# The sample group's cached keys are stored page by page, and the new keys get a buffer and a matmul of their own

## The reference, cut to what matters

```
# per sample: 512 cached keys (4 pages of 128, found by page_table) and 8 new keys
k_all = concatenate([past_k, k]); v_all = concatenate([past_v, v])
s = einsum(q, k_all) * DA_DK**-0.5 + bias        # 8 heads, 2 maps, 8 queries, 520 keys
p = softmax(where(dist >= 0, s, NEG_INF))
o = (p[:, 0] - lam * p[:, 1]) @ v_all            # then RMSNorm per head
```

## Time and profile before

| | us |
|---|---|
| median of 3 runs | 1562.69 |
| lowest and highest | 1562.01, 1567.64 |
| span of the profiled execution | 1563.0 |
| PE busy in it | 1482.6 (95%) |
| DVE, ACT, POOL busy | 615.1, 468.7, 72.6 |

### The profile page before, as it was taken

One profiled execution on the slowest core, in us unless ns is written; L12 is line 12 of the kernel. 1 busy time (PEld: TensorE's weight loads), 2 busy tenths in 40 slices (PEclk: granted clock), 3 DMA queues, 4 the chain that ended last, 5 costly groups with the idle time before them and its releaser, 6 DMA issues.

```text
span 1563.0 us, 26015 instructions
## 1 busy us (share of the span) xinstructions
PE 1482.6 (95%) x10030; PEld 1337.4 (86%) x10030; DVE 615.1 (39%) x940; ACT 468.7 (30%) x817; POOL 72.6 (5%) x133
## 2 busy tenths in 40 slices
PE   4999999988799999999999999999999999999996
PEld 3999965535599999999999336999999999999995
DVE  5212222257832234533334443335634444443223
ACT  4222210026743323333334115333332222222221
POOL 2000010021100001200010000000000000000000
PEclk9999999999999999999999999999999999999998
DMA  5436178720112433123256640222222222223232
GB/s 186 141 103 227 54 226 250 237 75 21 40 55 81 137 96 103 54 81 122 83 209 182 232 155 1 81 81 85 77 81 81 81 87 87 81 81 95 81 94 74
DMA packets 78422, 171.79 MB, mean 110 GB/s; under 512 B 5565, under 2 KB 39613, under 8 KB 77350
## 3 DMA queue, kind: packets, MB, share of 16 engines
q1 hardware_dynamic: 76614, 164.05, 33.0%
q0 software_dynamic: 1760, 7.08, 1.3%
HBM read 161.65 MB, written 11.82 MB: 111 GB/s over the span
## 4 chain that ended last, share of the span: by engine, by line
PE 61%; issue 28%; DVE 5%; DMA 3%; ACT 1%; SPq 1%; POOL 0%; DVEq 0%; POOLq 0%; ACTq 0%
PE acc L1579 43%; PE ps L1702 4%; PE acc L1675 3%; PE ps L1866 2%; PE acc L1885 2%; PE ps L1750 2%; DMA w_raw<-w_stream 1%; DMA k_pg<-cache_k 1%; DVE logit_p L1139 1%; PE acc L1936 1%; PE acc L1771 1%; ACT w_hi L613 1%; DVE a_p L1159 1%; DVE w_lo L960 1%; PE acc L1761 1%
## 5 line engine op out<-in xcount | busy, mean ns | idle before, releaser
L960 DVE TENSOR_TENSOR w_lo<-w_raw,w_hi 128x1024 fp32r<-128x1024 f32 x188 | 231.0, 1229 | 590.8 <-ACT w_hi L613 590.2
L1579 PE MATMUL acc<-h_hi,w_hi 128*128 128x288 f32 x1856 | 399.7, 296 | 7.6 <-DVE h_lo L995 4.5
L1579 PE MATMUL acc<-h_lo,w_hi 128*128 128x288 f32 x1856 | 396.5, 294 | 0.0
L1579 PE MATMUL acc<-h_hi,w_lo 128*128 128x288 f32 x1856 | 396.3, 294 | 0.0
L613 ACT ACTIVATE w_hi<-w_raw 128x1024 fp32r<-128x1024 f32 x188 | 198.5, 1056 | 360.5 <-PE acc L1579 355.6
L1579 PEld LDWEIGHTS acc<-h_hi,w_hi 128*128 128x128 f32 x1856 | 297.2, 188 | 10.1 <-issue 5.2
L1579 PEld LDWEIGHTS acc<-h_hi,w_lo 128*128 128x128 f32 x1856 | 297.9, 188 | 0.0
L1579 PEld LDWEIGHTS acc<-h_lo,w_hi 128*128 128x128 f32 x1856 | 297.8, 188 | 0.0
L1579 PE MATMUL acc<-o_hi,w_hi 128*128 128x288 f32 x384 | 82.2, 295 | 2.0 <-ACT zmT L882 1.2
L1579 PE MATMUL acc<-o_hi,w_lo 128*128 128x288 f32 x384 | 82.1, 294 | 0.0
L1579 PE MATMUL acc<-o_lo,w_hi 128*128 128x288 f32 x384 | 81.7, 294 | 0.0
(11 more groups left out here) (242 smaller groups left out, 1576.7 us busy)
## 6 DMA issues: line engine op xcount, KB each, us to landing
w_raw<-w_stream SPq DMA_DIRECT2D x188, 512.0 KB, 3.5
v_pg<-cache_v SPq DMA_DIRECT2D x28, 512.0 KB, 4.7
k_pg<-cache_k SPq DMA_DIRECT2D x16, 512.0 KB, 6.3
k_odd<-cache_k SPq DMA_DIRECT2D x16, 512.0 KB, 6.4
km_pg<-mem_k SPq DMA_DIRECT2D x8, 1024.0 KB, 5.1
vm_pg<-mem_v SPq DMA_DIRECT2D x8, 1024.0 KB, 5.0
x_sb<-xT SPq DMA_DIRECT2D x8, 576.0 KB, 4.7
kT_out<-kT POOLq DMA_DIRECT2D x1, 2304.0 KB, 10.6
```

Source lines behind the costliest of these rows:

```text
L960: nc.vector.tensor_tensor(w_lo[:, u, :], w_raw[:, u, :], w_hi[:, u, :].bitcast(F32), ALU.subtract)\
L1579: last = nc.tensor.matmul(acc[a][:, c, 0:n], w[:, u, k * P:(k + 1) * P], x[:, k0 + k, c * n:(c + 1) * n], start=start and k == 0 and t == ...
```

## The change

Each key page becomes one run of 1024 elements (4 KB) in each partition: the buffer is now pages x heads x 128 keys. The 8 new keys of each head get a small buffer of their own. The scores of a head are one matmul of 512 columns over the four pages (its moving operand is four runs of 128 elements, 4 KB apart) into the first bank, and after all eight heads one matmul of 8 columns for each head into the second bank. The 520 scores are again contiguous, across the border of the two banks, and DVE reads them as one row. In full:

```diff
-        k_pg = da.take("k_pg", [P, HEADS, KEYS])
+        k_pg = da.take("k_pg", [P, PAGES, HEADS, PAGE])
+        kn_pg = da.take("kn_pg", [P, HEADS, TS])
...
-        k_odd = Region(x_at).take("k_odd", [P, HEADS, KEYS])
-        assert x_at + 4 * HEADS * KEYS <= h_at
+        odd = Region(x_at)
+        k_odd = odd.take("k_odd", [P, PAGES, HEADS, PAGE])
+        kn_odd = odd.take("kn_odd", [P, HEADS, TS])
+        assert odd.at <= h_at
         k_slot = (k_pg, k_odd)
+        kn_slot = (kn_pg, kn_odd)
...
-                    sp.dma_start(k_slot[e][:, :, j * PAGE:(j + 1) * PAGE],
+                    sp.dma_start(k_slot[e][:, j],
...
-                    nc.vector.tensor_tensor_reduce(out=logit_s[:, e, :].rearrange("p (c n) -> p c n", c=2),
-                                                   in0=acc[0][:, :, 0:HK],
-                                                   in1=bias_s[:, :].rearrange("p (c n) -> p c n", c=2),
+                    nc.vector.tensor_tensor_reduce(out=logit_s[:, e, :],
+                                                   in0=acc[0][:, :, :].rearrange("p c n -> p (c n)")[:, 0:KEYS],
+                                                   in1=bias_s[:, :],
...
-                nc.gpsimd.tensor_copy(k_slot[e][:, :, PAST:KEYS], kT[:, :, bass.ds(SEQ + b * TS, TS)]).then_inc(s_q, 1)
+                nc.gpsimd.tensor_copy(kn_slot[e][:, :, :], kT[:, :, bass.ds(SEQ + b * TS, TS)]).then_inc(s_q, 1)
...
-                    for c in range(2):
-                        last = nc.tensor.matmul(acc[0][:, c, 0:HK], q_blk[:, h, :], k_slot[e][:, h, c * HK:(c + 1) * HK],
-                                                start=h == 0, stop=h == HEADS - 1)
+                    nc.tensor.matmul(acc[0][:, 0, :].rearrange("p (j n) -> p j n", j=PAGES), q_blk[:, h, :],
+                                     k_slot[e][:, :, h, :], start=h == 0, stop=h == HEADS - 1)
+                for h in range(HEADS):
+                    last = nc.tensor.matmul(acc[0][:, 1, 0:TS], q_blk[:, h, :], kn_slot[e][:, h, :],
+                                            start=h == 0, stop=h == HEADS - 1)
```

## The result

| us | before | changed |
|---|---|---|
| median (runs), first comparison | 1565.16 (4) | 1576.34 (4) |
| lowest, highest | 1562.01, 1567.92 | 1573.61, 1579.49 |
| ratio | | 1.0080, 95% interval 1.0051 to 1.0110 |
| median (runs), second comparison | 1564.20 (23) | 1577.26 (6) |
| ratio | | 1.0079, 95% interval 1.0056 to 1.0102 |

The changed kernel is slower, by 11 to 13 us in the medians (the two intervals allow 8 to 17 us). The last row is the stretch in which the change works: from 186.79 to 333.99 us before, and from 186.42 to 343.95 after. That is 10.3 us more, and it holds nearly all of the difference.

The account below looks back on a forecast made before the run. The prediction took PE to bound the sample attention. 11.4 us of added score matmuls, less 2.0 of key waits and 0 from the clock, made +9.4 us: 1572.1 us, with a range of 1567.5 to 1577.

Parts of the forecast that it names:

- PE bounds the stretch: Sample attention: an added microsecond of PE work in samples 0 to 7 is an added microsecond of time.
- Removed, 7.21 us a sample: Old score matmuls: 32 records of 225.3 ns a sample go, 57.7 us over eight samples.
- Long matmuls, 429 ns a record and nothing for the runs: New 512-column score matmuls: 16 records, 6.86 us a sample; four-run operand costs nothing, at most 2.7 us in all.
- The 0.09 us of a group's start: Scores of a sample: extra for the first start behind another group, making 8.54 us into 8.63.
- Short matmuls, 105 ns a record: New 8-column score matmuls: 16 records a sample pay for their weight loads, 1.68 us, range 1.66 to 2.08.
- Waits for key pages, 2.0 us less: PE's waits ahead of samples 2 and 4, 1.58 and 0.41 us, go; they would go even at the old transfer speed.
- The clock's fall moves to sample 1: TensorE's drop to 1.2 GHz in sample 2's scores moves to sample 1 rather than going: 0 us from the clock.
- its first rival: Sample 2's scores: the clock's fall goes with the idle time, +7.7 us, 1570.4 us; chance 0.25.
- From the stretch to the median: Whole time: +9.4 us on the profiled span of 1563.0 gives 1572.4, then a median of 1572.1 us.
- I move it as much: Whole time: the runs' median, 1562.69, lies 0.3 us below the span, so the forecast is lowered by that.
- Short matmuls nearly free: 8-column matmuls: weights taken in early under the long ones, so the kernel is not slower, down to 1557.9 us; chance 0.04.

Follow-up runs that it names:

- e6: Changed kernel with the long matmuls' moving operand as one run of 512 elements instead of four of 128; 1578.25 us, ratio 1.0080 to the kernel before.
- e4: Changed kernel with one 8-column matmul per sample instead of eight, so seven heads' new-key scores are missing; 1565.07 us, ratio 1.0003 to the kernel before.
- e5: Changed kernel with 64 instead of 8 columns in each short matmul; 1574.85 us, ratio 1.0072 to the kernel before.
- e7: Changed kernel with short matmuls of 32 weight columns, heads in the order 0, 2, 4, 6, 1, 3, 5, 7; 1564.37 us, ratio 0.9993 to before.
- e3: Changed kernel with key loads in eight runs of 512 bytes as before; 1576.55 us, ratio 1.0075 to the kernel before.
- e2: Kernel before with only the new 4 KB key loads, its old score matmuls kept (keys and heads mixed up); 1562.99 us, ratio 0.9993.
- e1: The changed kernel run again without edit, beside the kernel before on the same chip; 1577.26 us, ratio 1.0079.
- e8: e7 with the long matmuls also cut to 32 weight columns, in the same head order; 1562.99 us, ratio 0.9981 to the kernel before.
- e10: e8 with only the transpose of a finished output moved behind the value matmuls; 1561.77 us, ratio 0.9983 to the kernel before.

## Why the prediction was right or wrong, step by step

The direction and the mechanism came true; what failed are two sizes: the short matmuls were priced too low, and the step from the stretch to the median started from a base that was too low. The second is the larger one.

- **PE bounds the stretch.** Right. The 10.3 us more of PE's work and waits show one to one as 10.3 us of the stretch.
- **Removed, 7.21 us a sample.** Right.
- **Long matmuls, 429 ns a record and nothing for the runs.** Right, by the steps of 429 ns and by e6. The 0.09 us of a group's start stands there too: 6.97 is 16 x 0.429 and 0.11 more.
- **Short matmuls, 105 ns a record.** The mechanism is right (e4, e5, e7), the size was not: 111 ns. This is the term of the sum that was mis-sized. The error lies in the reading of the earlier trace rows. 1.04 us over ten records is 104 ns only on average: the first step there is 30 ns and the other nine are 112 ns each, by the starts of the single records. The combination's 116 ns are a first step of 55 ns, six of 112 and a last one of 205 ns ahead of the next group, so its extra is not on the first start, as the prediction has it. The steady step is 112 ns with 1, 8, 64 and 128 columns alike. With 0.02 us more at the start of the long ones this makes 1.54 and not 1.42 us a sample, **0.9 us in all**: 12.3 us added, not 11.4.
- **Waits for key pages, 2.0 us less.** Right, and e3 bears out that the old form does as well there, with the fall of the clock in sample 1. The faster load has nothing to win once the scores are longer. Alone it won these waits and the fall in the stretch (e2). PE comes to sample 2's scores at 209.09 and not at 207.4, since that sum leaves out the fall that the prediction itself puts into sample 1; the 2.0 us do not hang on it.
- **The clock's fall moves to sample 1.** The place came true in the first profile, in e1, e3 and e7, and not in e5 and e6, where PE has nearly the same work. (The combination ahead of the old fall takes 204.60 - 203.39 = 1.21 us and not 1.25.) The reason given for it, that the short matmuls put more thin work ahead of the idle time, is not borne out: e7 has only 0.24 us of them and the fall comes, e5 and e6 have all of them and it does not. So that the fall stood where it was forecast is in part luck. Both the forecast and its first rival happen, and 1.7 us go one way or the other with the execution.
- **From the stretch to the median: the step that failed most.** +9.4 us was forecast for the stretch, +10.3 came. The time moved by 11.2 us in the first comparison and 13.1 in the second, with 8.8 us as the low end of the second's interval, so 10.3 is compatible with it. The predicted 1572.1 us is 4.2 below the measured 1576.34. Of these, 0.9 are the short matmuls. Another 2.5 lie in the step "I move it as much". It took three runs' median, 1562.69, as the base, 0.3 us below the profiled span, while these runs already spread over 5.6 us; the base measured beside the changed kernel was 1565.16. The later runs list span and time of each execution, and the time is always the longer one, by 1.7 to 1.8 us. So an execution with the span of 1563.0 us took about 1564.8 us (an estimate from these), and the three runs' median was low by chance. The step should have gone up by 1.8 us from the span, not down by 0.3.
- **What stays open.** The remaining 0.8 us, and up to 2 more by e1, are not traced to a place. The prompt attention and the rest behind it differed by 2.7 and 1.1 us between two executions of the changed kernel (first profile and e1), and it had one fall of the clock more in the longer one. Whether the changed kernel has more falls on average stays open. e1's median, 1577.26, is 0.3 us above the stated range: its top, 1577, was drawn around a base that was too low.
- **Short matmuls nearly free.** Out, 111 ns. As e7 shows, it comes true only with narrow weights on different strips.

## What to carry to other kernels

In this kernel a float32 matmul record with a weight load of 128 columns of its own paid the larger of its columns and its load: 429 ns with 512 columns, 225 with 260, and 112 with 128, 64, 8 or 1. Splitting 520 columns into 512 and 8 instead of 260 and 260 keeps the count of loads and takes the cover from half of them; before such a split, multiply the short ones by the price of a load. And where only some rows of a weight tile are not zero, cut the tile to their strip of 32 columns and let neighbouring matmuls use different strips, as e7 and e8 do. Then look at once for what waits next: here nine tenths of the gain in the stretch (4.2 of 39.4 us came with e8) stayed away until the value pages were used and released one by one and the transpose stood behind the values. The transpose alone won nothing (e10).

## What the runs showed of the hardware

- Four float32 matmuls on four different strips of 32 output rows ran at four times the rate: 16 records of 512 columns in 1.74 us instead of 6.97, and 16 of 8 columns in 0.24 instead of 1.78 (e8, e7). The long ones start in rounds of four, and a round still takes 429 ns.
- Float32 matmul records with fresh 128-column weights start 112 ns apart, whether they have 1 column (the 1128 us rows of before), 8 (the changed kernel), 64 (e5) or 128 (the 349 us rows of before).
- A moving operand in four runs of 128 elements, 4 KB apart, streams as fast as one run (e6).
- One program's executions lie up to 9 us apart on this chip: 24 runs of the kernel before went from 1559.78 to 1568.85 us. Profiles of kernels with equal or nearly equal work (the changed kernel, e1, e3, e5, e6) differ by where, and how often, the clock falls to 1.2 GHz. Ahead of a fall stood idle times of PE of 1.3 to 3.1 us, and the same idle time did not always bring one: the 1.8 us ahead of sample 1 did in the changed kernel and not in e5 and e6.
